# Ropes of one attention ahead of another, expert sums above the down product, and the output by half tiles

## The reference, cut to what matters

```python
for l in range(2):
    h, hc = modulate(x, ...), modulate(xc, ...)
    z, zc = h @ w_in, hc @ w_in
    ya = differential attention      # "A": 4 heads of 32, two softmaxes each, keys with grid rope
    yb = long convolution            # Hyena
    yc = windowed attention, sinks   # "C": 4 heads of 64, 2 key heads, grid rope
    yd = Conformer convolution
    y  = sum_b sigmoid(z @ gate_b + bias) * (y_b @ w_branch[b]) @ w_out
    x  = x + g1 * y
    x  = x + g2 * moe(modulate(x, ...))   # top-1 group, top-2 of its 4 experts, 16 experts
```

## Time and profile before

| | us |
|---|---|
| median of 3 runs | 1601.78 (1601.4 to 1606.16) |
| the profiled execution: its own time | 1604.79 |
| its span, first to last instruction | 1603.1 |
| PE busy in the span | 1491.4 (93%) |
| DVE, ACT, POOL busy | 598.5, 288.9, 93.4 |
| mean granted TensorE clock | 0.972 |
| stretch of attention A in layer 0 | about 281 to 412 |
| attention C in layer 0 | about 415 to 505 |
| experts of layer 0 | about 677 to 956 |
| experts of layer 1 | about 1370 to 1594 |
| DMA rate of 1390 to 1550 in windows of 20 | 419 to 428 GB/s, DMA share 1.00 to 1.03 |

### The profile page before, as it was taken

How to read it: one execution, slowest core, us unless ns; L and a number is a source line. 1 busy time by engine, 2 the same in 40 slices (tenths; PEclk the granted TensorE clock), 3 DMA queues, 4 the chain that set the end, 5 groups by cost and what they waited for, 6 DMA issues and landing times.

```text
span 1603.1 us, 17603 instructions
## 1 busy us (share of the span) xinstructions
PE 1491.4 (93%) x6666; PEld 748.4 (47%) x6666; DVE 598.5 (37%) x1502; ACT 288.9 (18%) x596; POOL 93.4 (6%) x107
## 2 busy tenths in 40 slices
PE   5999999997999999799999997999989997999987
PEld 2544554443444444533333324755767874433332
DVE  4277633566532222512122124653665314211101
ACT  3211111332232301311111112110232302000000
POOL 0000010000101100000000001001001110000000
PEclk8999999999999999899999998999989998999999
DMA  9347321241312132499999966473232347899995
GB/s 370 137 173 272 132 78 53 80 150 61 131 53 83 53 157 73 165 350 407 415 408 411 412 244 236 177 280 138 89 131 79 132 185 299 332 424 421 424 422 207
DMA packets 38178, 354.53 MB, mean 221 GB/s; under 512 B 4272, under 2 KB 4656, under 8 KB 16976
## 3 DMA queue, kind: packets, MB, share of 16 engines
q1 hardware_dynamic: 30784, 329.73, 52.0%
q0 software_dynamic: 4016, 14.24, 2.4%
q10 hardware_dynamic: 3296, 9.44, 1.5%
HBM read 342.83 MB, written 10.56 MB: 220 GB/s over the span
## 4 chain that ended last, share of the span: by engine, by line
PE 62%; DVE 5%; DMA 4%; ACT 2%; issue 1%; SPq 1%; POOL 0%; DVEq 0%; PEldq 0%; ACTq 0%; POOLq 0%
PE ps L1347 18%; PE ps L1059 16%; PE ps L1357 5%; PE ps L1240 5%; PE ps L1157 3%; PE ps L1069 3%; DMA gates<-w 2%; PE ps L1369 1%; PE ps L1040 1%; DMA mr<-w 1%; PE ps L1019 1%; PE ps L1193 1%; PE ps L1335 1%; PE ps L1186 1%; PE ps L1229 1%
## 5 line engine op out<-in xcount | busy, mean ns | idle before, releaser
L1059 PE MATMUL ps<-hT,ring 128*128 128x512 f32 (+1 forms) x1344 | 452.6, 491 | 1.5 <-DVE hT L2071 1.5
L1059 PEld LDWEIGHTS ps<-hT,ring 128*128 128x128 f32 x1344 | 254.8, 192 | 177.3 <-issue 154.6
L1347 PE MATMUL ps<-ring,m 128*64 128x512 f32 x528 | 239.2, 604 | 9.7 <-DMA n_<-w 3.8
L1347 PEld LDWEIGHTS ps<-ring,m 128*64 128x64 f32 x528 | 70.0, 139 | 159.0 <-issue 150.3
L1069 PE MATMUL ps<-ring,hT 128*128 128x512 f32 (+1 forms) x352 | 126.0, 516 | 3.6 <-DMA ring<-win 3.6
L1157 PE MATMUL ps<-yT,ring 128*128 128x512 f32 (+1 forms) x256 | 96.0, 498 | 4.5 <-ACT n_ L1675 4.5
L1069 PEld LDWEIGHTS ps<-ring,hT 128*128 128x128 f32 x352 | 66.4, 190 | 62.3 <-issue 58.1
L1240 PE MATMUL ps<-ring,wide 128*128 128x512 f32 x192 | 83.1, 593 | 0.8 <-POOL wide L1822 0.8
L1349 PE MATMUL ps<-n_,m 128*64 128x512 f32 x176 | 82.0, 621 | 0.0
L1634 ACT ACTIVATE gates<-ps,hbg 128x512 f32<-128x512 f32 (+1 forms) x64 | 37.2, 581 | 247.7 <-PE ps L1059 185.2
L1349 PE MATMUL ps<-wide,m 128*64 128x512 f32 x176 | 79.6, 598 | 0.0
(11 more groups left out here) (362 smaller groups left out, 1769.1 us busy)
## 6 DMA issues: line engine op xcount, KB each, us to landing
ring<-w SPq DMA_DIRECT2D x40, 2048.0 KB, 10.8
ring<-wmod SPq DMA_DIRECT2D x24, 2048.0 KB, 8.5
ring<-win SPq DMA_DIRECT2D x24, 2048.0 KB, 8.1
n_<-w SPq DMA_DIRECT2D x13, 2048.0 KB, 14.7
hT<-w SPq DMA_DIRECT2D x13, 2048.0 KB, 17.7
wide<-w SPq DMA_DIRECT2D x13, 2048.0 KB, 15.6
ring<-wbr SPq DMA_DIRECT2D x8, 1024.0 KB, 4.8
ring<-wout SPq DMA_DIRECT2D x4, 2048.0 KB, 7.9
```

The source lines that it names most:

```text
L1059: last = pe.matmul(b[:, 0:W], w[:, k, jj * P:(jj + 1) * P], hT[:, k, 0:W], start=(k == 0), stop=(k == KD - 1))
L1347: pe.matmul(ps[0:HALF, bnk, :], left[:, k, 0:HALF], even[k], start=(k == 0), stop=(k == n_k - 1), skip_group_check=True)
```

## The change

In layer 0 `rsC` and the four `ropeC` leave the second half of attention A and join the work that stands among the first 12 gate groups (12 side groups before, 17 after; 54 side groups in the stretch of attention A before, 49 after). Layer 1 keeps its order. In the experts of layer 1 `mix(e - 1)` moves from between the gate and the up product to between `turn_u` and the down product. In both layers the load of the count moves from the end of the experts to behind pair 0. After each of the first three half tiles of the last `mix` TensorE signals (`half_mixed`), `mixgate` waits for that alone, and x is added and stored by half tiles (512 of 1024 columns).

```diff
-    o += merge(conformer[:12], prepared("A") + projections)
+    turns = [g for g in prepared("C") if g[0][0] == "T"]
+    ropes = [[("V", ("rsC", l))]] + [g for g in prepared("C") if g[0][0] == "V"]
+    early_ropes, late_ropes = (ropes, []) if l == 0 else ([], ropes)
+    o += merge(conformer[:12], prepared("A") + projections + early_ropes)
     units = attention("A")
     half = len(units) // 2
-    turns = [g for g in prepared("C") if g[0][0] == "T"]
-    ropes = [[("V", ("rsC", l))]] + [g for g in prepared("C") if g[0][0] == "V"]
     o += settled(spread(conformer[12:] + spread(gate_groups(1, False), ahead),
-                        units[:half] + spread(units[half:], ropes) + turns))
+                        units[:half] + spread(units[half:], late_ropes) + turns))
...
             o += [("V", ("mixgate", l, t, hf))]
-        o += [("V", ("xup2", l, t))]
+            o += [] if with_side(l) else [("V", ("xhalf", l, t, hf))]
+        o += [("V", ("xup2", l, t))] if with_side(l) else []
...
             for t in range(2):
-                sp.wait_ge(vector_done, vector("xup2", DEPTH - 1, t))
-                sp.dma_start(out[t * P:(t + 1) * P, :], x[:, t, :]).then_inc(out_stored, 16)
-            sp.wait_ge(out_stored, 32)
+                for half in range(2):
+                    at = slice(half * 512, half * 512 + 512)
+                    sp.wait_ge(vector_done, vector("xhalf", DEPTH - 1, t, half))
+                    sp.dma_start(out[t * P:(t + 1) * P, at], x[:, t, at]).then_inc(out_stored, 16)
+            sp.wait_ge(out_stored, 64)
...
+                                if last_ and signal and (t, half) != (live(l) - 1, 1):
+                                    last.then_inc(half_mixed, 1)
...
-                        if not side and e:
-                            mix(e - 1)
                         weights_landed("w3", e)
...
                         turn_u(e)
+                        if not side and e:
+                            mix(e - 1)
...
-                    for e in range(PAIRS):
+                    pair(0, True)
+                    count = assignments(pe, l)
+                    for e in range(1, PAIRS):
                         pair(e, e < PAIRS - 1)
...
-                    count = assignments(pe, l)
                     with pe.If(count > room(l)):
...
-                        v.wait_ge(tensor_done, tensor("experts", l))
+                        if (t, half) == (tt - 1, 1):
+                            v.wait_ge(y_mixed, PAIRS)
+                        else:
+                            v.wait_ge(half_mixed, 2 * t + half + 1)
...
+                elif kind == "xhalf":
+                    t, half = rest
+                    at = slice(half * 512, half * 512 + 512)
+                    last = v.tensor_tensor(x[:, t, at], x[:, t, at], xn[:, t, at], ALU.add)
+                    last.then_inc(vector_done, 1)
```

More of the change, by code:

```diff
@@ L734, in build_trunk @@
         y_mixed = sem("y_mixed")
+        half_mixed = sem("half_mixed")
         side_gathered = sem("side_gathered")
@@ L1364, in split_k, with mix_block @@
                         return [(even, 0, 0, whole), (odd, 0, SIDE, whole), (even, 4, 0, whole), (odd, 4, SIDE, whole)]
-                    def mix_block(first, last_):
+                    def mix_block(first, last_, signal=True):
                         for t in range(live(l)):
@@ L1515, in _ @@
                                 pe.wait_ge(more_vector[l], n_block * 4 + 4)
-                                mix_block(False, True).then_inc(more_tensor[l], 1)
+                                mix_block(False, True, False).then_inc(more_tensor[l], 1)
                         if not side:
@@ L1790, in _ @@
                     pair(0, True)
+                    count = assignments(act, l)
                     with act.Fori(1, PAIRS - 1) as e:
@@ L1795, in _ @@
                         act.wait_ge(y_stored, (base + PAIRS) * 16)
-                    count = assignments(act, l)
                     with act.If(count > room(l)):
@@ L1847, in _ @@
                     for e in range(0 if side else 1, PAIRS):
+                        if e == 1:
+                            count = assignments(gp, l)
                         if e:
@@ L1878, in gather_y @@
                                   .then_inc(y_gathered[t], 16)
-                    count = assignments(gp, l)
                     more = more_blocks(l)
@@ L2528, in _ @@
                     pair(0, True)
+                    count = assignments(v, l)
                     if side:
@@ L2535, in _ @@
                     pair(PAIRS - 1, False)
-                    count = assignments(v, l)
                     steps = 4 if side else 5
@@ L2562, in _ @@
                             v.tensor_copy(ysb.rearrange("p (a n) -> p a n", a=2), results).then_inc(more_vector[l], 1)
+                        if not side:
+                            v.wait_ge(tensor_done, tensor("experts", l))
                     v.nop().then_inc(vector_done, 1)
```

## The result

The changed kernel takes 1620.18 us (median of 5 runs, 1617.73 to 1620.66), the kernel before beside it 1606.16 (5 runs, 1601.4 to 1608.7): ratio 1.009, 95% interval 1.0074 to 1.0106, some 14 us slower. The profiled executions have spans of 1603.1 and 1616.6, so **+13.5** is to be explained. The direction was forecast, the size was not: 1611 was predicted, and 1620 lies above the range.

What follows compares the result with a forecast made beforehand. PE, busy 93%, was taken as the bound: nearly every idle microsecond lengthens the span. Terms 10.5 - 0.8 + 3.0 - 3.5 = +9.2 put the profiled execution at 1614, less 3.0 for the median: 1611, range 1599 to 1617.

Steps and rivals of the forecast that it cites:

- Long stall, early ropes: Layer 0 attention A: PE's 7.69 wait, made by ropeC(1), goes; ropes in front take 14.4 and fit with 0.7 to spare.
- the rival of late ropes: Early ropes take 18.0 as measured before and are late: another 2.9, perhaps a clock loss, 1614 to 1617; 10%.
- The new waits: Layer 0 attention A: shifted groups make PE wait at yA, yR, transposes and a gate; 19.1 against 10.6, 8.5 more.
- The walk: Following attention A's queues on paper with trace durations; gave 10.0 for the old order's 10.6, so good to about 1.
- The clock: Lower clock behind attention A's stalls: two clusters at 1.6 each, single waits nothing, 1.2 given back: +2.0 net.
- the far end of 15: Upper end of the +10.5 for ropes, new stalls and clock in attention A; the lower end was 5.
- Out of layer 0's experts: Leaving layer 0's experts: the count's load moves under pair 0's matmuls, saving 0.8, between 0 and -1.2.
- Expert sums: Layer 1, last pair: mix behind turn_u delays down by 2.3, plus 0.7 for the clock: +3.0, ends 1.6 and 4.2.
- Tail: Kernel's end: VectorE ends 3.3 sooner behind the last mix, smaller last store 0.2: -3.5, ends -3.0 and -4.0.
- the rope stall simply goes: Rival: attention A's long stall vanishes and new ones are hidden; -9.8 in all, 1592; 14%.
- The stalls cancel: Rival: attention A's new stalls come to about 10 to 12 with little clock loss; 1601 to 1606; 14%.

Runs made afterwards that it cites:

- the ropes at their old places: Against the kernel before: attention A's other steps in the order the change leaves, each rope put back before the step it preceded; 1621.86 us, ratio 1.0115.
- the ropes alone: Against the kernel before: only the ropes move forward in layer 0; experts, count and tail as before; 1617.83 us, ratio 1.0083.
- the last pair kept: Against the kernel before: mix(e - 1) of layer 1 moved above the down product except in the last pair; 1606.61 us, ratio 1.0021.
- the order kept: Against the kernel before: ropes run in front, every other step of attention A keeps its place of before; 1598.71 us, ratio 0.9961.
- the walked order: Against the kernel before: ropes in front, attention A's other steps placed by walking queues on paper until no wait exceeds 0.6; 1590.41 us, ratio 0.99.
- the sums alone: Against the kernel before: only mix(e - 1) of layer 1 moves, from before the up product to before the down product; 1609.97 us, ratio 1.0035.

## Why the prediction was right about the sign and wrong about the size

**Long stall, early ropes: right.** The 7.69 went. From 273.63 to 288.67 the ropes took 14.3 and one `gmul` 0.72, 14.4 was forecast for the ropes, and the first maxima began at 289.42 (forecast margin 0.7; the rival of late ropes did not happen). With no `gadd` beside them they took the short durations: 4.3 for the rope of a latent tile, where the earlier trace rows has 5.25. The Trainium skill, "SBUF — State Buffer", section "Who interferes with whom", says that a VectorE instruction with two SBUF inputs contends with a GpSimd instruction that reads SBUF; the trace agrees, since GpSimd did nothing from 267 to 293 and the operation that had taken 1.25 took 0.29.

**The new waits: right, one by one.** Forecast and measured (the figure behind a name is the tile, `pT(1,1)` is tile 1, head 1): `yA0` 2.6 and 2.50, `yR0` 0.3 and 0.27, pT(1,1) 3.6 and 3.41, late `pA` 1.0 and 0.76, `yA1` 1.2 and 1.42, `yR1` 2.5 and 2.35, gate(1,4) 2.4 and 2.54, `yM2` 0.3 and 0.26, `yR2` 2.2 and 2.06, `yR3` 3.0 and 2.93. Their sum is 18.5 for 19.1, and the step from before to after 7.9 for 8.5. The run with the ropes at their old places shows that these waits come from the order. The walk is not always that close: it gave 6.8 for the old stall of 7.7, and in that run 0.4 for a wait of 1.26.

**The clock: the step that failed.** The waits and their places were right; the term "+2.0 net" for the clock was too small. It charged 1.6 to each of two clusters, nothing to the three single waits, and gave 1.2 back for the rope stall. Attention C begins 13.1 later, 13.4 from the start of the stretch; less the waits that is 5.5 for the 2.0. The window rows say where: the cluster at 366 to 369 cost 2.8 (5.69 of work at half the clock), and the single waits of 2.06 and 2.93 cost 1.7 each; the cluster at 333 to 336 and the single wait of 2.50 at 319 cost nothing. On the other side, the lower clock of the kernel before lay to more than half inside the stall, and gave back 1.5 only. That is 6.3 less 1.5, 4.8 of the 5.5; 0.7 stays unassigned. Charging "none for the single waits" erred, and the far end of 15 did hold the 13.4.

Which wait is followed by the lower clock is not settled by the order. With the ropes alone, the same waits as in the full change, the cluster at 333 did cost 1.7 and the wait of 2.05 nothing. The gates behind the two, first in the full change and then with the ropes alone:

```profile
336.64 7.03 PE L1064 MATMUL ps<-hT,ring 128*128 128x512 f32 x16
...
398.58 8.73 PE L1064 MATMUL ps<-hT,ring 128*128 128x512 f32 x16
```

```profile
336.77 8.73 PE L1060 MATMUL ps<-hT,ring 128*128 128x512 f32 x16
...
399.51 7.03 PE L1060 MATMUL ps<-hT,ring 128*128 128x512 f32 x16
```

The totals are alike all the same: 12.5 from the start of the stretch, less 7.7 of waits, 4.8 there for the 5.5 here. So it was the sum of the term that failed, not one choice in it, and why one wait is followed by the lower clock and its twin is not stays open. The Trainium skill, "TensorE: Matmul & The Clock Gate", section "HAM oscillation — how this bites in real kernels", tells it of waits on DMA, after which work starts at the lower clock; here some of the waits of 2 to 3 on VectorE and ScalarE did the same.

**Out of layer 0's experts: wrong, small.** -0.8 was forecast; the last pairs of layer 0 run 14.0 later than before and layer 1's experts begin 13.9 later (1376.81 for 1362.95), so -0.2, with several stretches of the lower clock between that fell otherwise. PE's own start moved as forecast, from 2.54 to 1.59 (the load was thus 0.95 of the 2.54, not most of it), but the first gather came 0.6 further from the last down product, where 0.8 nearer was forecast. What was missed is that the gathers wait for the store, and the store for a packet of code.

**Expert sums: right in place and nearly in size.** From that landmark the last `mix` is 3.5 later (17.34 less 13.86), 3.0 forecast. 1.7 of it is the lower clock in the up product (from its start to `turn_u` 9.63 for 7.95), for which 0.7 was added; the rest is 1.8 for 2.3. No weight came earlier for it, and the pairs in the middle do not count, as the run with the last pair kept shows.

**Tail: right.** -3.8 for -3.5, by the local reading.

**The sum.** 13.4 less 0.3 for an earlier start of the stretch, 0.7 between 428 and 1377, 3.5 and -3.8 make the 13.5 of the spans. Forecast was 9.2. Of the 4.3 between, the clock behind attention A makes 3.5, the way from 428 to 1377 (0.7, where the exit from layer 0's experts was to give -0.8) 1.5, and the other terms come to -0.7. As much again, 4.9, has to do with the level and not with the change: the 1620.18 is 1.9 above the profiled execution, and 3.0 was taken off because the profiled execution of before ran that much above the median of 1601.78 of three runs. With two more runs this median is 1606.16, and medians beside the experiments are 1603 to 1605. The same sum on 1606.16 would have given 1615.

**The rivals.** That the rope stall simply goes happened in one sense: with the order kept, the gain was -6. The condition named for it, `yM` in front of a gate, is what the walked order fulfils. In the changed kernel it did not hold. "The stalls cancel" fell with the 18.9.

## What to carry to other kernels

When groups are laid evenly among others, taking some out moves all that stand behind them: make the move and keep the positions, or lay them out anew, and don't take the one for the other. Walk the queues of the new order on paper with the durations of the trace; here that found every wait of the changed kernel within 0.3, and turned round it found an order worth 1%. Where waits of 2 to 3 on TensorE are added, allow for the lower clock behind each of them, also when it stands alone: here a single one cost 0 or 1.7 and a cluster 0 to 2.8, and the sum over them was steadier than any one (about 5 net in two traces). Don't credit the removal of a long stall with a loss of clock that lay inside the stall.

## What the runs showed of the hardware that was not expected

The same instructions with the same waits do not lose the same by the clock. In the run with the sums alone, attention A is the kernel before to 0.1 in every wait, and yet behind the 7.70 its gate took 9.71, where the earlier trace rows has 8.28:

```profile
390.75 0.69 PE L1193 MATMUL ps<-con,n_ 128*128 128x128 f32 x2 [7.70 <-ACT n_ L1675]
391.23 9.71 PE L1059 MATMUL ps<-hT,ring 128*128 128x512 f32 x16
```

The pair of traces with the new order (7.03 and 8.73 behind the same wait, and the other way round behind the other) shows the same. By layer 1's experts the run with the sums alone was 7.1 behind, with nothing changed ahead of them. Differences of a few us between two single executions of this kernel are therefore no evidence. From landmark to landmark they are only where the clock can be read beside them.

With a single packet of code (queue q8, 1.0 to 1.7 us on one of the 16 DMA engines) among the packets of two stores of 128 KB, the stores landed 0.5 to 0.8 later, in six traces of six, and the gather behind them up to 1.6; in the eight traces without it neither happened.
